# Two edits in a two-block transformer kernel: routing of an expert layer with constant products in TensorE's waits and the first job's tokens in halves, and a program end by token blocks with the last norm's weights multiplied in first

## The reference

```python
for l in range(DEPTH):                      # DEPTH = 2
    x = x + hybrid_mixer(rmsnorm(x, norm_mix[l]), ...)
    x = x + hierarchical_moe(rmsnorm(x, norm_ffn[l]), w_router_group[l], ..., w_gate[l], w_up[l], w_down[l])
return rmsnorm(x, norm_final)
```

## Time and profile before

| | |
|---|---|
| median of 3 runs | 1988.84 us (1987.57 to 1989.27) |
| the profiled execution's own time | 1984.64 us |
| its span in the trace | 1982.8 us |
| mean granted TensorE clock | 0.982 of full |
| PE busy | 1830.4 us (92%) |
| DVE, ACT, POOL busy | 862.0, 762.5, 73.5 us |
| moved by DMA | 549.01 MB, mean 277 GB/s |

### The profile page before, as it was taken

One profiled execution on the slowest core, in us unless ns is written; L12 is line 12 of the kernel. 1 busy time (PEld: TensorE's weight loads), 2 busy tenths in 40 slices (PEclk: granted clock), 3 DMA queues, 4 the chain that ended last, 5 costly groups with the idle time before them and its releaser, 6 DMA issues.

```text
span 1982.8 us, 28956 instructions
## 1 busy us (share of the span) xinstructions
PE 1830.4 (92%) x10170; PEld 1154.0 (58%) x10170; DVE 862.0 (43%) x1644; ACT 762.5 (38%) x1387; POOL 73.5 (4%) x97
## 2 busy tenths in 40 slices
PE   7899999998999999979999999998979999999996
PEld 6679998875799988854333333336964333333333
DVE  4776566568765566952111111114882111111113
ACT  5454334546543345523233233234532323323323
POOL 3300000110000000000000000000010000000000
PEclk9999999998999999989999999999989999999999
DMA  8545554460355545329999999997508999999994
GB/s 298 198 155 177 185 191 153 155 191 33 116 186 181 186 148 192 106 79 411 422 422 422 422 422 422 422 422 273 183 19 324 422 422 422 422 422 422 422 422 184
DMA packets 154037, 549.01 MB, mean 277 GB/s; under 512 B 10639, under 2 KB 70249, under 8 KB 105577
## 3 DMA queue, kind: packets, MB, share of 16 engines
q1 hardware_dynamic: 150368, 539.20, 70.3%
q0 software_dynamic: 3088, 8.10, 1.2%
q10 hardware_dynamic: 504, 0.66, 0.1%
HBM read 546.81 MB, written 1.11 MB: 276 GB/s over the span
## 4 chain that ended last, share of the span: by engine, by line
PE 50%; DMA 37%; DVE 6%; ACT 3%; issue 2%; POOL 1%; SPq 0%; ACTq 0%; DVEq 0%; POOLq 0%
DMA raw<-in_w_expert_down 36%; PE pb L1121 25%; PE pb L1665 6%; PE pb L1413 6%; PE pb L1635 2%; PE pb L1226 1%; PE pb L1249 1%; PE pb L1347 1%; PE pb L1602 1%; ACT parts L720 1%; PE pb L1272 1%; DVE parts L1788 1%; POOL rms L696 1%; PE pb L1711 1%; DMA raw<-in_w_in 1%
## 5 line engine op out<-in xcount | busy, mean ns | idle before, releaser
L1635 PE MATMUL pb<-raw,xw 128*64 128x512 f32 x2016 | 485.1, 604 | 6.5 <-ACT xw L995 5.3
L1788 DVE TENSOR_TENSOR parts<-raw,parts 128x2048 fp32r<-128x2048 f32 (+1 forms) x138 | 307.4, 2231 | 130.6 <-ACT parts L720 127.6
L720 ACT ACTIVATE parts<-raw 128x2048 fp32r<-128x2048 f32 (+1 forms) x138 | 256.7, 1866 | 225.5 <-PE pb L1121 163.3
L2371 DVE TENSOR_TENSOR qk<-qk,pb 128x256 f32<-128x256 f32 x126 | 52.8, 421 | 665.3 <-ACT qk L1005 665.3
L1121 PE MATMUL pb<-xT,parts 128*128 128x256 f32 (+1 forms) x2712 | 333.3, 283 | 0.0
L1121 PEld LDWEIGHTS pb<-xT,parts 128*128 128x128 f32 (+1 forms) x2712 | 329.2, 191 | 4.7 <-issue 2.9
L1665 PE MATMUL pb<-raw,qk 128*64 128x512 f32 x1008 | 242.4, 602 | 63.6 <-DMA raw<-in_w_expert_down 60.9
L1121 PE MATMUL pb<-parts,xT 128*128 128x512 f32 (+1 forms) x1200 | 272.2, 385 | 4.4 <-DVE xT L1799 3.9
L1635 PEld LDWEIGHTS pb<-raw,xw 128*64 128x64 f32 x2016 | 123.5, 136 | 232.2 <-issue 161.9
L1121 PEld LDWEIGHTS pb<-parts,xT 128*128 128x128 f32 x1200 | 218.0, 189 | 50.6 <-DVE xT L1799 4.7
L1665 PEld LDWEIGHTS pb<-raw,qk 128*64 128x64 f32 x1008 | 67.1, 136 | 236.7 <-issue 160.6
(11 more groups left out here) (303 smaller groups left out, 1360.8 us busy)
## 6 DMA issues: line engine op xcount, KB each, us to landing
raw<-in_w_expert_gate SPq DMA_DIRECT2D x126, 1024.0 KB, 12.6
raw<-in_w_expert_up SPq DMA_DIRECT2D x126, 1024.0 KB, 12.4
raw<-in_w_expert_down SPq DMA_DIRECT2D x126, 1024.0 KB, 12.7
raw<-in_w_ffn_gate SPq DMA_DIRECT2D x22, 1024.0 KB, 5.4
raw<-in_w_ffn_up SPq DMA_DIRECT2D x22, 1024.0 KB, 5.3
raw<-in_w_ffn_down SPq DMA_DIRECT2D x22, 1024.0 KB, 5.0
raw<-in_w_in SPq DMA_DIRECT2D x16, 1024.0 KB, 5.4
raw<-in_w_in_ab SPq DMA_DIRECT2D x12, 1024.0 KB, 12.1
```

The source lines that it names most:

```text
L720: nc.scalar.activation(parts[:, (SPL0[seg] + k) % SPL, 0, 0:kk * nn], raw[:, place, 0:kk * nn], ACT.Copy).then_inc(hi_done[seg], 1)
L1635: ins = mm(pb[m][rows, :], xw[:, 4 * hf + k, :], w[:, k, :], start=(hf == 0 and k < 2), stop=(hf == 1 and k >= 2))
L1788: v.tensor_tensor(two[:, 1, :], raw[:, place, 0:kk * nn], two[:, 0, :].bitcast(F32), ALU.subtract)\
L2371: v.tensor_tensor(d, d, pb[2 + m][:].rearrange("p (k i s) -> p k i s", k=4, i=2)[:, :, 1, :], ALU.add)\
```

## The change

Routing, on PE: `spin(n)` issues n products of a constant by a constant (128x128 by 128x256, float32) into PSUM bank 7, which nobody reads. Two stand inside the router's products ahead of a wait, ten behind them (ahead of the wait for `as_done`), three behind the job table's sums (ahead of the gather).

Routing, on DVE: the first token block's `sel` is made ahead of `tab`. The table's sums go to PSUM bank 3 instead of bank 1.

First job: the gather's banks are renumbered, so that PE's banks 0 and 1 are free after the first group. ACT copies the first job's tokens in two halves, each when its four channel groups are in `xsT`. PE takes gate half 0 and up half 0 after the first copy, gate half 1 and up half 1 after the second. `used` goes up by one, by nothing, by two and by one.

Back to tokens: in the second half of the columns, token block 0 is completed before block 1 is begun (before, the blocks took turns slot group by slot group).

Program end: the squares are made in four pieces of 512 columns, the first two when the first half of the sums is in `h`. DVE multiplies each block of `h` by the norm's weights while the root is not there yet, and scales by the root afterwards; ACT takes a quarter of that scaling. The output goes in three DMAs (512 KB, 256 KB, 256 KB), two from SP and one from ACT.

```diff
         def gather_bank(k):
-            return pb[4 + k] if k < 4 else pb[k - 4]
+            return pb[(0, 1, 4, 5, 6, 7, 2, 3)[k]]
...
@@ SP, end
-            sp.dma_start(out[0].rearrange("(t p) d -> p t d", p=P), xs[:]).then_inc(stored, 16)
-            sp.wait_ge(stored, 16)
+            sp.dma_start(out[0, 0:P, :], xs[:, 0, :]).then_inc(stored, 16)
+            sp.wait_ge(out_ready, 3)
+            sp.dma_start(out[0, P:S, 0:512], xs[:, 1, 0:512]).then_inc(stored, 16)
+            sp.wait_ge(stored, 48)
...
@@ POOL, last root
+                if last:
+                    pool.wait_ge(sq_done, 22)
+                    first = rms[:, R_FIRST:R_FIRST + 2]
+                    nc.gpsimd.tensor_scalar(first, first, 1.0 / D, EPS, ALU.mult, ALU.add).then_inc(pch, 1)
+                    pool.wait_ge(pch, r + 2)
                 pool.wait_ge(*wait)
                 a = rms[0:parts_n, col:col + n]
-                if width == D:
+                if last:
+                    nc.gpsimd.tensor_tensor(a, a, first, ALU.add).then_inc(pch, 1)
+                elif width == D:
...
@@ ACT, moe(l)
                     nc.scalar.activation(xsT[:, k, 0:NS], gather_bank(k)[:], ACT.Copy,
                                          scale=gperm[:, l, k:k + 1]).then_inc(xsT_a, 1)
-                act.wait_ge(xsT_a, 4 * (l + 1))
-                act.wait_ge(xsT_v, 5 * (l + 1))
+                    if k % 4 == 2:
+                        act.wait_ge(xsT_a, 5 * l + (2 if k == 2 else 5))
+                        act.wait_ge(xsT_v, 5 * l + (3 if k == 2 else 5))
+                        ins = nc.scalar.activation(xw[:, k - 2:k + 2, :], xsT[:, k - 2:k + 2, 0:W], ACT.Copy)
+                        ins.then_inc(xsT_a if k == 2 else xw_ready[l], 1)
...
@@ ACT, end
-            squares(10)
+            for c in range(2):
+                for t in range(NT):
+                    act.wait_ge(h_done, 39 + t if c else 38)
+                    col = (R_NORM[10] if c else R_FIRST) + t
+                    cols = slice(512 * c, 512 * (c + 1))
+                    nc.scalar.activation(xs[:, t, cols], h[:, t, cols], ACT.Square, scale=D ** -0.5 if c else 1.0,
+                                         accum_out=rms[:, col:col + 1]).then_inc(sq_done, 1)
+            act.wait_ge(out_ready, 1)
+            act.wait_ge(rstd_done, ROOT_AT[("norm", 10)])
+            nc.scalar.activation(xs[:, 1, 512:], hg[1][:, 512:], ACT.Copy, scale=rstd(10, 1)).then_inc(ach, 1)
+            act.wait_ge(ach, 1)
+            act.dma_start(out[0, P:S, 512:], xs[:, 1, 512:]).then_inc(stored, 16)
...
@@ PE
+            def spin(n):
+                for _ in range(n):
+                    mm(pb[7][:, 0:2 * P], ones[:], cst[:, 0:2 * P], start=True, stop=True)
...
                     if (k0, t) == (4, 0):
+                        spin(2)
                         wait_xT(10 + 3 * l)
...
                 ins.then_inc(rt_ready, 1)
+                spin(10)
...
+                mm(pb[3][0:1, 128:129], wm, ones[0:NE, 0:1], start=True, stop=True)
                 mm(pb[3][0:NE, 1:2], tri[0:NE, 0:NE], wm, start=True, stop=True)
...
-                mm(pb[1][0:1, 0:JOBS], ones[0:NE, 0:1], ja, start=True, stop=True)
-                mm(pb[1][0:1, 64:64 + JOBS], jv, jo, start=True, stop=True).then_inc(job_ready, 1)
+                mm(pb[3][0:1, 0:JOBS], ones[0:NE, 0:1], ja, start=True, stop=True)
+                mm(pb[3][0:1, 64:64 + JOBS], jv, jo, start=True, stop=True).then_inc(job_ready, 1)
+                spin(3)
...
-                step(0)
+                first = gate_up(0)
+                pe.wait_ge(xsT_a, 5 * l + 3)
+                products(0, *first[0])
+                products(0, *first[2], done=0)
+                pe.wait_ge(xw_ready[l], 1)
+                products(0, *first[1], done=2)
+                products(0, *first[3])
                 gates_turned()
...
+                for sc in range(4):
+                    for t in range(NT):
+                        into_tokens(0, t, sc)
+                    slots_turned(1, sc)
+                for t in range(NT):
                     for sc in range(4):
+                        into_tokens(1, t, sc)
+                    if t == 0 and l == 0:
+                        turn_half(8, 0)
...
@@ DVE, route(l): the three tab instructions, with their wait for job_ready, now stand here
                 for t in range(NT):
+                    if t:
+                        dve.wait_ge(job_ready, l + 1)
+                        link(v.tensor_scalar(tab[0:1, 0:JOBS], pb[3][0:1, 0:JOBS], float(NE - 1), None, ALU.min))
...
                     link(v.tensor_scalar(sel[:, t, :], i512, sl[0][:, t:t + 1], None, ALU.is_equal))
...
@@ DVE, end of moe(1) and of the program
                 add(1, 0)
+                if l:
+                    dve.wait_ge(h_done, 39)
+                    with_gain(0)
                 add(1, 1)
+                if l:
+                    dve.wait_ge(h_done, 40)
+                    with_gain(1).then_inc(out_ready, 1)
+                    dve.wait_ge(out_ready, 1)
...
-            for t in range(NT):
-                v.scalar_tensor_tensor(xs[:, t, :], h[:, t, :], rstd(10, t), gfin, ALU.mult, ALU.mult).then_inc(out_ready, 1)
+            v.tensor_scalar(xs[:, 0, :], hg[0], rstd(10, 0), None, ALU.mult).then_inc(out_ready, 1)
+            v.tensor_scalar(xs[:, 1, 0:512], hg[1][:, 0:512], rstd(10, 1), None, ALU.mult).then_inc(out_ready, 1)
```

More of the change, by code:

```diff
@@ L220, in build @@
         gfin = qkf[:, 0:D]
+        hg = [qkf[:, D * (t + 1):D * (t + 2)] for t in range(NT)]
         x_loaded = sem("x_loaded")
@@ L535, in build @@
         root(("mixed", 1), (yss_done, 2), R_ATT[1], 4, CW)
-        for n in range(9, 11):
-            root(("norm", n), (sq_done, 2 * n + 2), R_NORM[n], 2, D)
+        root(("norm", 9), (sq_done, 20), R_NORM[9], 2, D)
+        root(("norm", 10), (sq_done, 24), R_NORM[10], 2, D)
         PARS = []
@@ L1636, in products @@
                                  stop=(hf == 1 and k >= 2))
-                    ins.then_inc(used[seg], 1)
+                    if done:
+                        ins.then_inc(used[seg], done)
                 def turn(j, back, m, src, done):
```

57 lines of the change are left out of this document (26 added, 31 removed).

## The result

| | before | after |
|---|---|---|
| median | 1988.84 us (1987.57 to 1991.1, 5 runs) | 1977.72 us (1976.14 to 1979.59, 5 runs) |
| ratio, 95% interval | | 0.9945 (0.9934 to 0.9956) |
| profiled execution: own time, span | 1984.64, 1982.8 us | 1977.0, 1975.2 us |
| mean granted TensorE clock | 0.982 | 0.989 |

The change takes 11.1 us off the median (8.8 to 13.1 by the interval).

A forecast was written before the change was run, and what follows sets the result against it. The prediction took the unbroken DMA weight stream, placed by PE's start of job 0, to bound each expert layer, with serial stages outside. Terms -8.0 + 0.4 - 2.6 = -10.2 us gave a median of 1978.6, range 1973.5 to 1984.

The forecast's parts named there:

- Back to tokens: Layer 0's end: block 0 first needs the last slot pieces, so transposes and next projection come later, plus 0.4 us.
- Program end: After the last sums: shorter scaling chain and split output bring the last byte earlier, minus 2.6 us (bounds 1.8 to 3.2).
- The ten products: Routing, ahead of the counting: ten constant products fit PE's 5.98 us wait for DVE's choices and cost nothing.
- The three at the low level: Ahead of the gather: three constant products run at 1.2 GHz, end at 872.0, 0.3 us later than the gather started before.
- The stand of 2.7 us: Between gather and job 0: PE's wait for evacuations and token copy nearly vanishes through the halves, saving 2.4 us.
- I take 4.0 us a layer: Expert layers: earlier start of job 0 moves the weight stream forward 4.0 us each (bounds 3.2 to 5.6), 8.0 for two.
- the release comes 12.7 us after PE's start: Job 1: the ring place for the later load frees 12.7 us after job 0 begins, removing about 1 us of shortage.
- 1, the high level throughout: Routing: the 2.4 GHz clock holds from the ten to the gather, 5.6 us a layer, -13.4 in all, 1975.4; chance 0.14.
- 2, the ten at 1.2 GHz: Routing: the ten run slow throughout, counting starts 2.5 us late, -2.2 us in all, 1986.6; chance 0.05.
- 3, the stream doesn't follow PE: Job loop: grouped releases leave gaps costing what the early start gives, -2.2 us in all, 1986.6; chance 0.04.
- 4, output transfers pay their starts in a row: Program end: two more transfer starts and ends cost 3.6 us, -6.6 in all, 1982.2; chance 0.05.
- 5, slower: Routing: clock falls in the pause at 855.9 and stays low to the gather's end, +8 us in all, 1996.8; chance 0.05.

The follow-up runs named there:

- fill: Changed kernel with three more constant products between the gates' transposes and the one-column sums behind job 0; 1978.08 us, ratio 0.9951.
- no_const: Changed kernel without the fifteen constant products of each expert layer; 1978.29 us, ratio 0.9962.
- only_end: Kernel before with the new program end alone, including layer 1's tokens by blocks; 1984.14 us, ratio 0.998.
- no_three: Changed kernel without the three constant products ahead of the gather; 1977.98 us, ratio 0.995.
- best2: Changed kernel without the three constant products ahead of the gather and with layer 0's token blocks taking turns again; 1976.06 us, ratio 0.9939.
- whole_first: Changed kernel with the first job's tokens copied whole and its product halves in the old order, each adding one to `used`; 1982.11 us, ratio 0.9971.
- one_output: Changed kernel with the output in one 1 MB transfer issued by SP when all is scaled; 1975.88 us, ratio 0.995.

## Why the prediction was right, and where it wasn't

The forecast was 1978.6 and the median is 1977.72, in a range of 1973.5 to 1984.0. The mechanism stands: PE's start of job 0, with the speed of job 1's first products, sets the stream's place, and the stream the layer. From G2 to the last down product it is 456.96 us in layer 0 before and 457.07 after, and 442.09 and 441.64 in layer 1. But the terms don't all stand, and the near hit of the total is partly luck: the traces moved by 7.6 us where 10.2 were forecast, and the median by 11.1.

**Right.** The ten products at no cost: the wait ahead of the counting still ends at DVE's choices. The three at the low level, to 872.0: the gather starts at 872.12, 0.07 and 0.00 us relative later than before (0.3 forecast). The stand of 2.7 us gone to nothing: P0 lies 0.07 before the gather's last product ends, and P0 is 3.37 and 4.30 us earlier, where 3.9 was forecast. The stream's gap behind its first load is short, and where job 1 isn't slow the shortage after it is nearly gone (G2 - P0 12.86, 12.7 forecast; in layer 1 a window of 1 us from 1508 shows 295 GB/s, where two in a row from 1512 showed 139 and 336 before). Layer 1's term is -4.29, -4.0 forecast.

**The term that failed: layer 0's share of "I take 4.0 us a layer".** It came out at -1.80, outside the bounds of 3.2 to 5.6. The gather gave 0.56 instead of 1.5 us there (1.69 in layer 1), since the low level lasted 2.7 us into it and the rest took 6.5. The stand gave its part. Then 1.57 were lost between P0 and G2, in a place that I had taken as fixed, "the release comes 12.7 us after PE's start": job 1's first eight products ran at the low level. I had priced the clock around the products that the change adds, and nowhere behind them. The bounds should have held a low stretch in job 1, worth 1.1 to 1.7 us.

**Is it the change that brings the slow stretch?** It stood in 10 of 16 layers with the three products ahead of the gather (`fill` apart) and in 2 of 10 without them (none of 2 before, 1 of 2 in `no_const`, 1 of 2 in `only_end`, none of 4 in `no_three` and `best2`). The other layer of `only_end` lost as much in job 0 itself (G2 - P0 14.42), which makes it 3 of 10. That suggests it and doesn't show it. What is shown: it can come without them, it stood behind the one-column sums in 12 of 13 layers and at job 0's start in one, and moving the transposes does not remove it. Three products of 256 columns ahead of the sums were followed by none in two layers; two are too few to call that a cure. Why it comes in one execution and not in the next stays open. The Trainium skill, TensorE: Matmul & The Clock Gate, section "Part 1: The HAM clock gate (the "warmup" mystery)", says that where the clock changes is "run-variable" for one and the same kernel. The traces agree: the kernel after had the low stretch in one layer in one execution and in both in the other.

**Mis-sized.** Back to tokens: +0.66, forecast +0.4; the transposes start 2.02 us behind the start of the last low pieces, where I had 1.91, and before they started at 1.37, not at the 1.53 from which I counted. Program end: -2.17, forecast -2.6. The last sum's end comes 0.62 later against the last down product, not 0.35; POOL's addition takes 0.41, not 0.2; from the last sum's end to the root's it is 2.10, about as forecast. The scaling of 1024 columns took 0.75, inside its bound of 0.94.

**Where the other 3.5 us of median come from.** The terms of the two traces sum to -7.6, outside the median's interval of -8.8 to -13.1. The profiled execution before was a good one: 4.2 us below its median, as the prediction noted, while that after is 0.7 below. Over 41 runs of the kernel before, span and mean granted clock go together: 13 runs at 0.982 have a mean span of 1984.9 us, 10 at 0.980 one of 1987.7. The profiled one had 0.982 and 1982.8. The kernels that keep all constant products show 0.985 to 0.989, `no_const` 0.981 to 0.983. But the mean clock isn't time: `no_const`'s median is within 0.6 of the kernel after. Two pieces are traced. The prediction called the two products in the wait at 855.9 "hidden" and gave them no gain. In layer 0 of three kernels without them (before, `no_const`, `only_end`) the router's products behind the wait ran at 1.98, 2.90 and 3.25 us; in all 22 layers with them, and in layer 1 of the three kernels without, they ran at 1.98. So a loss of 0.9 to 1.3 us at the counting was seen in 2 of 6 layers without them and in none of 22 with them. Of these losses 0.9 us is left at P0 in `only_end` (36.30, before 35.43), and nothing in `no_const` (32.29, layer 1 32.48). The second piece is the slow stretches, of which the profiled execution before had none. In `only_end`, the one other execution traced with the old routing, G2 comes 2.45 and 0.83 us later than in it. Against that execution the two layers of the kernel after gain 9.4 us up to G2, against the profiled one 6.1. These 3.3 us are of the size of the missing 3.5, but one execution doesn't show that they are the same. The spread ahead of the first expert layer is as large: its first transposes stood anywhere from 846.4 to 851.0 us in kernels whose instructions are the same up to there.

**The rivals.** 1, the high level throughout: not in layer 0, nearly so in layer 1's gather (8.28 us), which gives its -4.3 but not -5.6, because the three products ahead of it still ran low. 2, the ten at 1.2 GHz: refuted, the window shows 1.00. 3, the stream doesn't follow PE: refuted by `whole_first` beside the kernel after. 4, output transfers pay their starts in a row: refuted by `one_output`, beside which the split gains 0.4 us. 5, slower: the fall of the clock in the pause at 855.9 that it begins with is real in kernels without the two products, and was not seen with them.

## What to carry to other kernels

A product of constants in a wait of PE is free only as long as the wait outlasts it (ten had 1.59 us to spare, twenty cost 2.66), and its worth is read two stages on, in the granted clock of what follows. The surest gain here was none of the clock: the first job's inputs in halves, so that PE begins without a stand, gave some 2 us a layer. In the 22 layers traced with halves PE went from the gather to job 0 without a stand, and in the 6 without them it stood 1.9 to 2.7 us. When single edits are worth less than the spread of the runs, compare distances between two named instructions within a stage, in several executions, and leave the medians for the whole.

## What the runs showed of the hardware that I had not expected

The granted clock of the same instructions differs between executions and layers. Sixteen products of 72 columns behind a wait of 1.37 us took 1.98, 2.90 or 3.25 us, eight of 512 columns behind the one-column sums 1.94, or 3.00 to 3.62, although PE was hardly idle around the latter. Idle time alone doesn't explain it: between 884 and 892 us PE waited 0.26 us in all in the kernel after, with the clock up, and then the clock fell.

A gather that starts 0.9 us earlier at the low level ended 0.2 us later on average than one that followed three constant products: work put ahead about paid its own time back (the 0.2 is less than the spread of either group, 31.68 to 32.24 and 31.04 to 32.42).

What one profile hides: the kernel before scatters with its mean clock, from 1987.7 us of span at 0.980 to 1984.9 at 0.982 on the mean of 10 and 13 runs, so a single trace of it can be several us from the median, and so can each term that is counted from it.
